# Paired attention with another order of VectorE's work, two chunks copied by ScalarE, and operand tiles at other byte offsets

## What is computed

```
def first_block(x, ...):
    h = rms_norm(x, norm1_g)
    z = jnp.einsum('bsd,dc->bsc', h, w_in)
    q_n, kc, vc, ksl, vsl, kwn, vwn, g_nsa, dil, mg = jnp.split(z, splits, axis=-1)
    y_nsa = nsa_attention(q_n, kc, vc, ksl, vsl, kwn, vwn, g_nsa, ...)
    y_dil = dilated_attention(dil, dil_q_norm, dil_k_norm)
    gm = jax.nn.sigmoid(mg.astype(jnp.float32)).reshape(B, S, 2, D)
    merged = gm[:, :, 0] * (y_nsa @ w_up_nsa) + gm[:, :, 1] * (y_dil @ w_up_dil)
    x = x + merged.astype(x.dtype) @ w_o
    return x + peer(rms_norm(x, norm2_g), peer_wq, peer_subkeys, peer_u, peer_v)
```

## Time and profile before

| | us |
|---|---|
| median of three runs | 3884.05 |
| the profiled execution | 3884.48 |
| its span in the trace | 3882.7 |
| TensorE busy | 3645.5 (94%) |
| TensorE weight loads | 3078.0 (79%) |
| VectorE busy | 2367.6 (61%) |
| ScalarE busy | 1414.6 (36%) |
| GpSimd busy | 404.2 (10%) |

### The profile page before, as it was taken

One profiled execution on the slowest core, in us unless ns is written; L12 is line 12 of the kernel. 1 busy time (PEld: TensorE's weight loads), 2 busy tenths in 40 slices (PEclk: granted clock), 3 DMA queues, 4 the chain that ended last, 5 costly groups with the idle time before them and its releaser, 6 DMA issues. The chain is left out here.

```text
span 3882.7 us, 47538 instructions
## 1 busy us (share of the span) xinstructions
PE 3645.5 (94%) x18133; PEld 3078.0 (79%) x18133; DVE 2367.6 (61%) x4176; ACT 1414.6 (36%) x2370; POOL 404.2 (10%) x309
## 2 busy tenths in 40 slices
PE   8988889999999989999998989999999898999998
PEld 6665667899999989999886767678867676777886
DVE  3365455698899988888635456544343546564433
ACT  3232224343599733333322224332222322443221
POOL 0020000000144434334000100000000001000000
PEclk9999999999999999999999999999999999999999
DMA  3220123355699999999532223223322222332322
GB/s 132 76 74 20 60 70 117 119 197 170 204 378 379 388 340 381 378 371 369 185 98 74 73 59 129 93 93 98 91 77 92 71 82 57 120 103 88 97 91 67
DMA packets 212358, 597.85 MB, mean 154 GB/s; under 512 B 21731, under 2 KB 79749, under 8 KB 210597
## 3 DMA queue, kind: packets, MB, share of 16 engines
q1 hardware_dynamic: 175268, 460.58, 35.8%
q0 software_dynamic: 36864, 134.23, 9.0%
HBM read 525.00 MB, written 69.21 MB: 153 GB/s over the span
## 5 line engine op out<-in xcount | busy, mean ns | idle before, releaser
L631 ACT ACTIVATE stream_hi<-stream_raw 128x1024 fp32r<-128x1024 f32 (+1 forms) x615 | 642.5, 1045 | 1237.3 <-PE ffn_ps L2740 435.4
L639 DVE TENSOR_TENSOR stream_lo<-stream_raw,stream_hi 128x1024 fp32r<-128x1024 f32 (+1 forms) x615 | 745.1, 1212 | 415.0 <-ACT stream_hi L631 407.9
L1209 PE MATMUL experts_ps<-mix_a_hi,stream_hi 128*128 128x384 f32 x1024 | 344.8, 337 | 19.4 <-issue 17.6
L667 PE MATMUL experts_ps<-h_hi,stream_hi 128*128 128x384 f32 x1024 | 349.7, 341 | 1.5 <-PEq L101 1.5
L667 PE MATMUL experts_ps<-h_hi,stream_lo 128*128 128x384 f32 x1024 | 345.0, 337 | 0.0
L667 PE MATMUL experts_ps<-h_lo,stream_hi 128*128 128x384 f32 x1024 | 345.0, 337 | 0.0
L1209 PE MATMUL experts_ps<-mix_a_lo,stream_hi 128*128 128x384 f32 x1024 | 344.6, 337 | 0.0
L1209 PE MATMUL experts_ps<-mix_a_hi,stream_lo 128*128 128x384 f32 x1024 | 344.6, 336 | 0.0
L2738 PE MATMUL mid_ps<-h_hi,stream_hi 128*128 128x512 f32 x672 | 288.6, 429 | 20.2 <-DVE h_lo L2767 17.1
L2738 PE MATMUL ffn_ps<-h_hi,stream_hi 128*128 128x512 f32 x704 | 287.5, 408 | 17.7 <-DVE h_lo L2767 17.7
L2739 PE MATMUL ffn_ps<-h_lo,stream_hi 128*128 128x512 f32 x704 | 279.6, 397 | 0.0
(11 more groups left out here) (464 smaller groups left out, 7144.9 us busy)
## 6 DMA issues: line engine op xcount, KB each, us to landing
stream_raw<-u SPq DMA_DIRECT2D x128, 512.0 KB
stream_raw<-v SPq DMA_DIRECT2D x128, 512.0 KB
stream_raw<-l_gu SPq DMA_DIRECT2D x88, 512.0 KB
expert_hidden<-experts_gelu SPq DMA_DIRECT2D x128, 192.0 KB
expert_weights<-built SPq DMA_DIRECT2D x12, 2048.0 KB
built<-expert_weights SPq DMA_DIRECT2D x16, 1536.0 KB, 13.1
built<-expert_hidden SPq DMA_DIRECT2D x128, 192.0 KB
stream_raw<-l_gate SPq DMA_DIRECT2D x48, 512.0 KB
```

The source lines that it names most:

```text
L631: self.nc.scalar.activation(self.hi[n % self.RING][:, 0:w], self.raw[n % self.RAW][:, 0:w], ACT.Copy).then_inc(self.hi_done, 1)
L639: self.nc.vector.tensor_tensor(self.lo[n % self.RING][:, 0:w], self.raw[n % self.RAW][:, 0:w], self.hi[n % self.RING][:, 0:w].bitcast(F32) ...
L667: mm = self.nc.tensor.matmul(self.ps[n % 2], a, b[:, k, :], start=(k == 0 and m == 0), stop=(k == DC - 1 and m == 2))
L1209: mm = nc.tensor.matmul(out[d][:, DIRECT:SEQ], v, a[b % RING][:, :], start=(b == 0 and m == 0), stop=(b == KEYS - 1 and m == 2))
```

## The change

Four things change. In nsa the new class `GatesByPair` moves the take of gate n from VectorE's work in unit n+1 to the end of unit n, behind its copies. In both stages the maxima, the exponentials' semaphore, the reciprocals, the gate weights and the scaling go by head: each head has an instruction and a step of the semaphore of its own, where one instruction served both. In dil ScalarE copies the first two of a unit's three chunks (`by_scalar` = 2) ahead of the exponentials of the next unit, and VectorE the third; nsa has `by_scalar` = 0. And four small tiles that nothing uses are allocated, which moves the tiles above them. The core of the diff (the semaphore `copied` becomes `copied_s` and `copied_v`, and `copied_after` names the one to wait for):

```
-def paired_attention(nc, name, C, pairs, scale, cols, ps, beside):
+def paired_attention(nc, name, C, pairs, scale, cols, ps, beside, by_scalar):
...
+        def copied_after(g):
+            n = max(j for j in range(N) if before[j] <= g)
+            c = g - before[n]
+            if c < by_scalar:
+                return copied_s, n * by_scalar + c + 1
+            return copied_v, before[n] - n * by_scalar + c - by_scalar + 1
...
                 def largest(n):
...
-                    steps.after(V.tensor_reduce(to, of, AX_X, ALU.max, negate=True))
-                    V.tensor_scalar(bias[n % 2][:, :, :], top[n % 2][:, :, :], scale, None, ALU.mult).then_inc(max_done, 1)
+                    for u in range(SIDES):
+                        of = scores[:, u, :].rearrange("p (k c) -> p k c", k=K)[:, :, 0:width]
+                        steps.after(V.tensor_reduce(top[n % 2][:, u, :], of, AX_X, ALU.max, negate=True))
+                        V.tensor_scalar(bias[n % 2][:, u, :], top[n % 2][:, u, :], scale, None, ALU.mult).then_inc(max_done, 1)
...
                 def weigh(n):
-                    dve.wait_ge(exp_done, n + 1)
...
                     for u in range(SIDES):
+                        at = SIDES * n + u + 1
+                        dve.wait_ge(exp_done, at)
+                        V.reciprocal(rden[n % 2][:, u, :], den[n % 2][:, u, :]).then_inc(inverted, 1)
...
-                    for c in range(chunks[n]):
+                    for c in range(by_scalar, chunks[n]):
                         copy(n, c)
-                beside.vector(dve, N)
+                    beside.after(dve, n)
...
+                    S.activation(probs_t[g % RING][0:rows, 0:width], turned[g % 2][0:rows, 0:width], ACT.Copy).then_inc(copied_s, 1)
...
                     beside.scalar(act, n)
+                    for c in range(by_scalar):
+                        copy(n, c)
                     if n + 1 < N:
                         exps(n + 1)
...
+class GatesByPair(GatesByUnit):
+    def vector(self, dve, n):
+        self.gates.stream.low(dve, self.gates.at(self.slots[n]) + 2)
+
+    def after(self, dve, n):
+        self.gates.take(dve, self.slots[n])
...
+        right("right_place", [P, 56])
+        base.enter_context(nc.sbuf_tensor("left_place", [P, 40], F32))
...
+            st.sb("ring_place", [P, 48], side="right")
...
+                    place.enter_context(nc.sbuf_tensor("next_place", [P, 56], F32, side="right"))
```

More of the change, by code:

```diff
@@ L439, in largest @@
                     if n >= 2:
-                        dve.wait_ge(exp_done, n - 1)
+                        dve.wait_ge(exp_done, SIDES * (n - 1))
                     width = pairs[n].parts[0][1]
-                    of = scores if K == 1 else scores.rearrange("p u (k c) -> p u k c", k=K)
-                    of = of[:, :, 0:width] if K == 1 else of[:, :, :, 0:width]
-                    to = top[n % 2][:, :, 0] if K == 1 else top[n % 2][:, :, :]
-                    steps.after(V.tensor_reduce(to, of, AX_X, ALU.max, negate=True))
@@ L448, in weigh @@
                 def weigh(n):
-                    dve.wait_ge(exp_done, n + 1)
                     if n >= 2:
[L451 to L456, removed]
-                    else:
-                        dve.wait_ge(inverted, n + 1)
@@ L459, in weigh @@
-                    by = (wgt if weighted else rden)[n % 2]
-                    for u in range(SIDES):
+                        dve.wait_ge(scaled, SIDES * (n - 1))
+                    for u in range(SIDES):
+                        at = SIDES * n + u + 1
+                        dve.wait_ge(exp_done, at)
+                        V.reciprocal(rden[n % 2][:, u, :], den[n % 2][:, u, :]).then_inc(inverted, 1)
+                        dve.wait_ge(inverted, at)
+                        if weighted:
+                            V.tensor_tensor(wgt[n % 2][:, u, :], rden[n % 2][:, u, :], pairs[n].weights[:, u, :],
+                                            ALU.mult).then_inc(weights_done, 1)
+                            dve.wait_ge(weights_done, at)
+                        by = (wgt if weighted else rden)[n % 2]
@@ L470, in copy @@
                         dve.wait_ge(chunk_mixed, g - RING + 1)
-                    rows, width = (pairs[n].extra[0].shape[1], P) if c < extra else (P, SIDES * P * len(blocks_of(n, c)))
-                    V.tensor_copy(probs_t[g % RING][0:rows, 0:width], turned[g % 2][0:rows, 0:width]).then_inc(copied, 1)
+                    rows, width = shape_of(n, c)
+                    V.tensor_copy(probs_t[g % RING][0:rows, 0:width], turned[g % 2][0:rows, 0:width]).then_inc(copied_v, 1)
                 largest(0)
@@ L495, in exps, with copy @@
                                                bias=bias[n % 2][:, u, k:k + 1], scale=scale, accum_out=den[n % 2][:, u, k:k + 1])
-                    ins.then_inc(exp_done, 1)
+                        ins.then_inc(exp_done, 1)
+                def copy(n, c):
+                    g = before[n] + c
+                    act.wait_ge(turn_done, g + 1)
+                    if g >= RING:
+                        act.wait_ge(chunk_mixed, g - RING + 1)
+                    rows, width = shape_of(n, c)
+                    S.activation(probs_t[g % RING][0:rows, 0:width], turned[g % 2][0:rows, 0:width], ACT.Copy).then_inc(copied_s, 1)
                 def store(n):
@@ L531, in sync @@
     def sync(self, sp):
+        pass
+    def after(self, dve, n):
         pass
@@ L2458, in dilated @@
                 dst=y_dil[:, n, at]))
-    paired_attention(nc, "dil", C, pairs, HD ** -0.5, 768, ps, beside)
+    paired_attention(nc, "dil", C, pairs, HD ** -0.5, 768, ps, beside, 2)
 def first_constants(shared, const1, masks):
@@ L2506, in attention_part @@
                     dst=y_nsa[:, n, at]))
-        paired_attention(nc, "nsa", C, pairs, HD ** -0.5, 1024, ps, GatesByUnit(merge_gates, {n: n for n in range(N_MERGE_GATES)}))
+        paired_attention(nc, "nsa", C, pairs, HD ** -0.5, 1024, ps, GatesByPair(merge_gates, {n: n for n in range(N_MERGE_GATES)}), 0)
 def up_and_out(nc, name, C, stream, y_nsa, y_dil, x, gains, h_hi, h_lo, x_rstd, gate_dram, gate_stored):
```

21 lines of the change are left out of this document (12 added, 9 removed).

## The result

The kernel after takes 3793.91 us (median of four runs, 3793.5 to 3798.59), beside 3884.8 for the kernel before on the same chip (3883.69 to 3888.21). The ratio is 0.9767, with a 95% interval of 0.975 to 0.9784: 91 us less, where 69 were forecast with an end of the range at 84. The profiled execution has a span of 3791.7 us (before 3882.7).

What follows compares the result with a forecast made beforehand. TensorE, busy 94% of the span, was taken to bound the kernel. From 3884.48 us, 39 for attention (31 nsa, 8 dil) and 30 for offsets gave 3815 us; range 3800 to 3855.

Steps and rivals of the forecast that it cites:

- the offsets: Whole kernel: moving operand tiles placed at 32 instead of 192 or 128 of 256 bytes shorten matmuls; 30 us.
- the stationary side: Stream tiles, TensorE's stationary operand, going from 224 to 32 for 14,376 matmuls: taken as nothing, ends -14 and +50 us.
- the split by head in dil: First paired stage: one reduce becomes two, with doubled small steps; covered by VectorE's slack, priced at nothing.
- the gaps in nsa: Second paired stage: TensorE's 15 waits for VectorE's take of the gate before would go; 23.5 us.
- The forecast's own floor: Matmuls of 512 columns with the moving tile at 32: median 392 ns, 229.1 ns from start to start.
- The rival that the stationary side pays: Stationary tiles lose 2 to 3.5 ns at 32 on 14,376 matmuls: 3845 to 3866 us; chance 0.20.
- The rival of 1 ns more: Stationary tiles gain too, 1 ns a matmul: 3801 us; chance 0.04.
- The slower case beyond it: The stationary tile's place costs 7 ns a matmul, 101 us in all: 3916 us, slower; chance 0.04.
- the halved attention: Rival: attention in dil and nsa gives half, with ScalarE the chain and copies late: 3835 us; chance 0.14.
- Offsets without effect: Rival: tile addresses do nothing, what looked like an offset is the stage: 3845 us; chance 0.06.
- The clock's part: In nsa, five gates that start at half clock behind the gaps would run warm; 7.9 us.
- The cover: In nsa's tightest case, VectorE's work behind the last copy fits before the next copy with about 1 us to spare.

Runs made afterwards that it cites:

- the attention alone: The kernel after without its four small tiles: attention as changed, all tile offsets as in the kernel before; 3840.61 us, ratio 0.9885.
- ring at 224: The kernel after with the ring of stream tiles (TensorE's stationary operand) back at 224 of 256 bytes, moving tiles left at 32; 3807.79 us, ratio 0.9807.
- the ring moved first: The kernel after with only the stationary stream tiles moved to 32, moving tiles at their old places; 3837.8 us, ratio 0.9877.
- The ring at 160: The kernel after with the stationary stream tiles at 160 of 256 bytes and moving tiles at 32; 3841.33 us, ratio 0.9883.

## Why the prediction was wrong, and where it was right

The sign and the parts were right, the size was not: 91 us where the range ended at 84. Of the 22 us between forecast and result, 13 are in the offsets (43.0 for 30), 4.6 in the attention alone (43.6 for 39), and 4.4 appear only with both together, within the noise. By dil and nsa themselves, read from mix to mix, the attention gave 47 us, 8 more than forecast; the span of the attention alone shows 3 less, of which 2.3 are in the experts' stage (see above). Three terms were sized wrong: the stationary side (0 for 14), the split by head in dil (0 for 2.9), and the gaps in nsa (23.5 for 26.6). The first alone would have left the time at 3801, just inside the range; it took the others to leave it.

**Offsets: 30 forecast, 43.0 us of span measured. The step that failed is "I take nothing for it", on the stationary side.** The comparison under it was of moving tiles at 32, 128 and 192, all over one stationary place, 224; it could not tell a place from a distance, and I read it as a place. The runs show the distance. The forecast's own floor, 392 ns or 229 from start to start, was the value at distance 64; the moving tiles alone do reach it (ring at 224: 228.6 and 228.8), and the ring's move, which makes the distance 0, brings the last 2 ns, 13.9 us in the whole time. The gain of the moving tiles was priced rightly for the ring at 224 (attention alone 3840.61, ring at 224 3807.79: 33 us, for 30 forecast). But the two sides are no terms of a sum at all: with the ring moved first, it gives 2.8 us, and the moving tiles behind it 43.9.

**The rival that the stationary side pays** (0.20) rested on one pair of rows, 399 against 396. It is refuted by the time, which fell when the ring moved, and the pair of rows is explained: with the ring at 224 the first block's stream-moving products have 399 at distance 192 over h at 32, and from start to start they stand at 235.9 where mid's stand at 233.3 over the same two places. Distance and places are the same, so the difference is the stage, which is what the prediction had offered as the other explanation. The rival of 1 ns more (0.04) had the right sign, and on 14,376 matmuls the right sum, 14 us, but by luck: it is 2 ns on those of 512 columns and nothing on the experts' 6144. The slower case beyond it (0.04) falls with it, and so does the halved attention (0.14): both halves of the attention gave more than was forecast.

**Offsets without effect** (0.06), where the Trainium skill leads ("SBUF — State Buffer", "Who interferes with whom", which counts TensorE's two read ports, for the moving operand and for the weights, as independent): refuted by the four small tiles alone, 41.1 us less of TensorE's busy time with not one instruction changed. What the page says under "Operand start alignment" is of legality and not of speed, by its own words, and no run here speaks against it.

**The take: 23.5 us forecast for the waits, 23.9 measured.** The clock's part was 7.9 for the gates and is 8.1. What the prediction left out are the modelled ends of the masks: it took a gap at its listed idle time, and by the starts each costs 0.18 us more, 2.7 in all. nsa in all gave 34.3 us with the take alone and 36.0 after, for 31 and an upper end of 34. The cover was said to be about 1 us; it is 2.1 to 2.9 (VectorE's idle time ahead of the first copy), and the doubled steps cost nothing in nsa, as priced.

**Dil: the step that failed is "Priced at nothing" for the split by head.** The reason given for it was nsa's (nothing waits there); for dil there was none. The price of ScalarE's copies was a little high too: I took VectorE's 0.69 us for 128x512 from PSUM, and the sixteen here take 592 to 597 ns, the second starting 0.49 us behind the first:

```profile
301.58 1.08 ACT L513 ACTIVATE dil_probs_t<-first_ps 128x512 f32<-128x512 f32 x2 [3.28 <-PE first_ps L409]
...
302.23 0.66 PE L425 MATMUL first_ps<-dil_probs_t,v_tok 128*64 128x128 f32 x8 [0.25 <-ACT dil_probs_t L513]
302.26 0.95 DVE L454 TENSOR_REDUCE dil_top<-first_ps 128x1 f32<-128x768 f32 x1
302.55 0.91 ACT L503 ACTIVATE dil_probs<-first_ps,dil_bias 128x768 f32<-128x768 f32 x1
```

In this unit the transposes start at 300.94, the mixing at 302.23: 1.29 us behind them (2.87 in the unit of the usual kind in the earlier trace rows, 1.4 forecast). The exponentials start at 302.55, 1.6 us behind the transposes and right behind the copies, while VectorE still reduces the other head's scores: without the split they would wait for both heads. That is the 2.9 us which I had put at nothing. dil from first to last mix gained 11.2 us, where 8 were forecast with ends of 2 and 12; ScalarE's copies without the split give 7.3, so that term was right.

**What was to show it.** No wait for the take, and a mixing 1.3 us behind the transposes: as said. A clock near 1.00 in nsa: 0.98. Medians of 392: 389. The experts at 336: 334, with no gain from start to start (173.4 and 173.6 ns for h2), so a median of durations there says nothing of the time.

Left open: each tile's own change of spacing, on the steps of 150 to 245 ns alone, adds up to 44 us for the four small tiles, and the span gave 43.0, so that sum closes. The ring at 160 loses 56 us by the same count, and the span 47; what takes back the rest was not followed. No run says what it is in TensorE's two operands that the distance acts on, nor what makes the second pattern at 64. Nor does any run say why a distance of 64 is better than 32.

## What to carry to other kernels

When one tile's time seems to depend on its address, look at the pair of operands: a row with the other operand somewhere else is what tells a place from a distance, and if the trace has none, the unknown side belongs in the range with both signs. Put the operation that frees a single buffer directly behind the engine's last piece of work for the present unit, and check who waits for what it pushes back; when such gaps go, more comes back than their listed idle time: here 8 us, since the matmuls behind them run at the full clock again, and 3 us of modelled ends. A split that shortens a unit of work pays only where the next engine in the chain is free to begin early.

## What the runs showed of the hardware that I had not expected

- Two fp32r matmuls of 512 columns in a row, each with its own weight load, start 226.7 ns apart when the moving and the stationary tile lie at the same address modulo 256 bytes, and up to 234.3 ns apart otherwise: 3.4%. At distance 0 the place itself (0, 32, 128) doesn't matter. With 384 columns a distance of 64 costs nothing and one of 128 costs 2.3 ns.
- At a distance of 64 a long row of such matmuls can also run at 233.3 ns, over the same tiles that otherwise run at 229.0; small matmuls in between put it back.
- The modelled duration of a matmul followed this spacing with 512 columns (392 to 389 for 229.0 to 226.7), but in the experts it fell by 2 ns where the spacing didn't fall.
- Of two copies of 128x512 from PSUM to SBUF in a row, ScalarE's second started 0.49 us behind the first (0.59 a record), VectorE's 0.61 (0.69 a record).
